# The factor of each RMS norm in a three-layer decoder kernel: square root and reciprocal instead of logarithm and exponential

## The reference

```python
def rmsnorm(x, gain):
    xf = x.astype(jnp.float32)
    y = xf * lax.rsqrt(jnp.mean(xf * xf, axis=-1, keepdims=True) + NORM_EPS)
    return (y * gain.astype(jnp.float32)).astype(x.dtype)
```

## Time and profile before

| | |
|---|---|
| median of 3 runs | 2280.27 us (2279.29 to 2281.51) |
| profiled execution | 2277.27 us |
| its span | 2275.5 us |
| mean granted clock of TensorE | 0.981 |
| busy: PE / DVE / ACT / POOL | 2178.8 / 1092.6 / 767.3 / 1146.0 us |
| share of the chain that ended last: PE / DVE / ACT | 84% / 9% / 3% |

### The profile page before, as it was taken

The page is one execution under the profiler, slowest core; times in us unless marked ns, Lnnn a source line. Parts: engine busy times, 40 slices in busy tenths (PEclk is TensorE's granted clock), DMA queues, the critical chain, the costliest instruction groups (busy, mean ns, idle before and its releaser), DMA issues.

```text
span 2275.5 us, 25960 instructions
## 1 busy us (share of the span) xinstructions
PE 2178.8 (96%) x9850; PEld 1803.8 (79%) x9850; DVE 1092.6 (48%) x1258; ACT 767.3 (34%) x850; POOL 1146.0 (50%) x817
## 2 busy tenths in 40 slices
PE   7999989999999999999999999979999799999996
PEld 5888768888888778978888888768887688888885
DVE  6255645555322356543545522774557655453224
ACT  5223343222123344543222223313565432222232
POOL 4465426555554433326555545535555455555554
PEclk9999999999999999989999999989999899999998
DMA  4211102322233222213232232222222222222331
GB/s 165 75 62 50 56 25 107 108 93 92 94 109 120 74 75 74 70 42 130 93 106 97 92 108 95 93 74 92 93 92 75 90 93 92 97 106 92 111 109 49
DMA packets 30198, 203.16 MB, mean 89 GB/s; under 512 B 3252, under 2 KB 3508, under 8 KB 6200
## 3 DMA queue, kind: packets, MB, share of 16 engines
q1 hardware_dynamic: 30136, 202.29, 25.0%
HBM read 200.18 MB, written 2.10 MB: 89 GB/s over the span
## 4 chain that ended last, share of the span: by engine, by line
PE 84%; DVE 9%; ACT 3%; issue 2%; POOL 0%; DMA 0%; DVEq 0%; ACTq 0%; SPq 0%; POOLq 0%
PE bank L1451 83%; DVE x L1340 1%; ACT L584 1%; ACT rstd L584 1%; DVE aqk L1211 1%; DVE x L1403 1%; DVE m_hi L1415 0%; DVE h L1350 0%; DVE rot L1210 0%; POOL ssq L570 0%; DVE un L1209 0%; ACT w_hi L584 0%; ACT s_a L584 0%; PE bank L1704 0%; DVE un L954 0%
## 5 line engine op out<-in xcount | busy, mean ns | idle before, releaser
L496 POOL TENSOR_TENSOR w_lo<-raw,w_hi 128x512 fp32r<-128x512 f32 x680 | 988.8, 1484 | 962.5 <-ACT w_hi L584 962.5
L1451 PE MATMUL bank<-u_hi,w_hi 128*128 128x512 f32 x1952 | 773.9, 396 | 38.9 <-DVE u_lo L958 15.1
L1451 PE MATMUL bank<-u_lo,w_hi 128*128 128x512 f32 x1952 | 764.1, 391 | 0.0
L584 ACT ACTIVATE w_hi<-raw 128x2048 fp32r<-128x2048 f32 x187 | 357.7, 1913 | 872.0 <-PE bank L1451 867.6
L1451 PE MATMUL bank<-u_hi,w_lo 128*128 128x512 f32 x1952 | 487.0, 389 | 0.0
L1451 PEld LDWEIGHTS bank<-u_hi,w_hi 128*128 128x128 f32 x1952 | 369.5, 189 | 122.9 <-issue 26.2
L1451 PEld LDWEIGHTS bank<-u_lo,w_hi 128*128 128x128 f32 x1952 | 369.4, 189 | 77.8 <-issue 2.6
L1451 PEld LDWEIGHTS bank<-u_hi,w_lo 128*128 128x128 f32 x1952 | 366.6, 188 | 76.4
L1451 PE MATMUL bank<-act_hi,w_hi 128*128 128x512 f32 x528 | 205.4, 389 | 0.0
L1451 PE MATMUL bank<-act_lo,w_hi 128*128 128x512 f32 x528 | 205.4, 389 | 0.0
L979 DVE TENSOR_TENSOR h<-h,bank 128x512 f32<-128x512 f32 x48 | 32.8, 683 | 304.3 <-PE bank L1451 304.3
(11 more groups left out here) (237 smaller groups left out, 2235.9 us busy)
## 6 DMA issues: line engine op xcount, KB each, us to landing
raw<-wall SPq DMA_DIRECT2D x187, 1024.0 KB, 4.8
h<-x_t SPq DMA_DIRECT2D x4, 512.0 KB, 6.9
out_t<-h SPq DMA_DIRECT2D x2, 512.0 KB, 2.8
out_t<-h SPq DMA_DIRECT2D x4, 256.0 KB, 3.0
lmask_f<-lmask_in SPq DMA_DIRECT2D x1, 512.0 KB
cs<-cs_in SPq DMA_DIRECT2D x1, 512.0 KB, 3.5
pf<-p_t SPq DMA_DIRECT2D x1, 512.0 KB, 3.5
amask<-amask_in SPq DMA_DIRECT2D x1, 256.0 KB
```

The source lines that it names most:

```text
L496: ins = nc.gpsimd.tensor_tensor(w_lo[:, s, c], raw[:, s, c], w_hi[:, s, c].bitcast(F32), ALU.subtract)
L584: return nc.scalar.activation(out, in_, func, **k)
L1451: return nc.tensor.matmul(out, lhsT, rhs, start=start, stop=stop, skip_group_check=True)
```

## The change

Each factor is now made by one Sqrt on ACT (`norm_root`) and one reciprocal on DVE (`norm_scale`, in place, DVE). The reciprocals stand in DVE's list right ahead of the first use; for m = 0 and 2 the small one of `rcol` comes first, and ACT takes the root of `rcol` ahead of that of `rstd`. The per-head factors of the recurrence (`root(hd)`) keep their Ln and Exp. The diff, cut to its core:

```diff
-            def norm_scale(m):
+            def root_of_mean(out, total):
+                return af(out, total, ACT.Sqrt, bias=eps[:, 0:1], scale=1.0 / DM)
+
+            def norm_root(m):
                 act.wait_ge(ms_ready, m + 1)
                 if m == TWIN:
-                    ch.link(af(rstd2[:], MS[:], ACT.Ln, bias=eps[:, 0:1], scale=1.0 / DM))
-                    af(rstd2[:], rstd2[:], ACT.Exp, scale=-0.5).then_inc(r4_ready, 1)
+                    root_of_mean(rstd2[:], MS[:]).then_inc(root_ready, 1)
                     act.wait_ge(t5_ready, 1)
-                    ch.link(af(rstd[:], sq[:, 0, :], ACT.Ln, bias=eps[:, 0:1], scale=1.0 / DM))
-                    af(rstd[:], rstd[:], ACT.Exp, scale=-0.5).then_inc(r5_ready, 1)
+                    root_of_mean(rstd[:], sq[:, 0, :]).then_inc(root_ready, 1)
                     return
-                ch.step(af(rstd[:], MS[:], ACT.Ln, bias=eps[:, 0:1], scale=1.0 / DM))
                 if m in (0, 2):
-                    ch.step(af(rcol[:], PB[5][:, 0:2 * TT], ACT.Ln, bias=eps[:, 0:1], scale=1.0 / DM))
-                ch.settle()
-                af(rstd[:], rstd[:], ACT.Exp, scale=-0.5).then_inc(rstd_ready, 1)
-                if m in (0, 2):
-                    ch.link(af(rcol[:], rcol[:], ACT.Exp, scale=-0.5))
+                    root_of_mean(rcol[:], PB[5][:, 0:2 * TT]).then_inc(rcol_root, 1)
+                root_of_mean(rstd[:], MS[:]).then_inc(root_ready, 1)
...
+            def norm_scale(m):
+
+                if m in (0, 2):
+                    dve.wait_ge(rcol_root, m // 2 + 1)
+                    ch.step(nc.vector.reciprocal(rcol[:], rcol[:]))
+                    ch.settle()
+                dve.wait_ge(root_ready, m + 1 if m < TWIN else m + 2)
+                nc.vector.reciprocal(rstd[:], rstd[:]).then_inc(rstd_ready, 1)
+                dve.wait_ge(rstd_ready, m + 1)
+
             def ffn(f, r, m):
-                dve.wait_ge(rstd_ready, m + 1)
+                norm_scale(m)
...
-            dve.wait_ge(r4_ready, 1)
+            dve.wait_ge(root_ready, TWIN + 1)
+            ch.link(nc.vector.reciprocal(rstd2[:], rstd2[:]))
             ch.link(tt(sq[:, 0, :], rstd2[:], rstd2[:], ALU.mult))
             tt(sq[:, 0, :], sq[:, 0, :], PB[5][:], ALU.mult).then_inc(t5_ready, 1)
             ch.link(nc.vector.memset(xpad[:, :, 0:3], 0.0))
-            dve.wait_ge(r5_ready, 1)
+            dve.wait_ge(root_ready, TWIN + 2)
+            ch.link(nc.vector.reciprocal(rstd[:], rstd[:]))
             ch.link(tt(rstd[:], rstd[:], rstd2[:], ALU.mult))
             dve.sem_inc(rstd_ready, 1)
```

More of the change, by code:

```diff
@@ L279, in build @@
         sg_ready = sem("sg_ready")
-        r4_ready = sem("r4_ready")
+        root_ready = sem("root_ready")
         t5_ready = sem("t5_ready")
-        r5_ready = sem("r5_ready")
+        rcol_root = sem("rcol_root")
         fin_ready = sem("fin_ready")
@@ L646, in ffn @@
                     if s == 0:
-                        norm_scale(m)
+                        norm_root(m)
                     act.wait_ge(sgin_ready, FT * f + s + 1)
@@ L669, in _ @@
             conv(1)
-            norm_scale(0)
+            norm_root(0)
             def sigmoids(p):
@@ L693, in by_tokens @@
                 conv(p0 + 2)
+                act.wait_ge(rstd_ready, 1)
                 for t in range(TT):
@@ L792, in values @@
                 act.wait_ge(tok_done, TT * (2 + g) + c + 1)
+                if c == 0:
+                    act.wait_ge(rstd_ready, 3)
                 k = (TT if g else 0) + c
@@ L814, in _ @@
                 if t == 0:
-                    norm_scale(2)
+                    norm_root(2)
                 halves(0, t)
@@ L876, in _ @@
                 if t == 0:
-                    norm_scale(TWIN)
+                    norm_root(TWIN)
             with act.Fori(0, KC // 2) as i:
@@ L931, in _ @@
                 if q == 0:
-                    norm_scale(6)
+                    norm_root(6)
                 for c in range(2):
@@ L939, in _ @@
                 squares(7, j)
-            norm_scale(7)
+            norm_root(7)
         @block.vector
@@ L1058, in _ @@
             cp(lmask[:], lmask_f[:]).then_inc(masks_ready, 1)
-            dve.wait_ge(rstd_ready, 1)
+            norm_scale(0)
             def both_scaled(n, t, ready, before):
@@ L1250, in _ @@
             dve.wait_ge(cs_loaded, 16)
-            dve.wait_ge(rstd_ready, 3)
+            norm_scale(2)
             for a in range(2):
@@ L1419, in _ @@
             ffn(2, 6, 5)
-            dve.wait_ge(rstd_ready, 7)
+            norm_scale(6)
             for q in range(4):
@@ L1442, in _ @@
             dve.wait_ge(gained, KC)
-            dve.wait_ge(rstd_ready, 8)
+            norm_scale(7)
             for j in range(OUT_SPLIT):
```

## The result

The changed kernel takes 2286.03 us in the median of 11 runs (2281.21 to 2290.35), the kernel before 2280.28 (2272.08 to 2282.32). The ratio is 1.0027, 95% interval 1.0018 to 1.0036: slower by 4 to 8 us. A second set of 12 runs gave 2287.02 against 2280.19, ratio 1.0032 (1.0020 to 1.0044).

A forecast was written before the change was run, and what follows sets the result against it. PE bounds the kernel (84% of the chain), so ACT and DVE count only where PE waits or only DVE remains. 1.2 + 1.6 + 1.4 + 1.2 + 0.2 = +5.6 us on 2280.27 gives 2285.9; 8-in-10 range 2281.5 to 2290.0.

The forecast's parts named there:

- The four norms behind which PE or the end waits: Costs at m = 2 (+1.2, clock +1.6), m = 4 (+1.4), m = 7 (+1.2) and m = 0 (+0.2).
- the four that are covered: Norms m = 1, 3, 5, 6: +1.2 us each against 2.9 spare, so no cost.
- The length of a reciprocal: A 128x512 reciprocal on DVE, R, put at 3.1 us between bounds of 0.73 and 5.6.
- the three ways to read the 203 ns: Fixed start from small operation or product, or excess spread over seven columns: R = 2.9 to 3.2, or 3.25 us.
- The short reciprocal: Rival: R = 0.73 us on DVE makes the kernel faster, -4.6 us, 2275.7; chance 0.09.
- the long one: Rival: R = 4.3 us, some 8 ns a column on DVE, +11 us, 2291; chance 0.13.
- The bound of 1.6: At m = 4, POOL may hold up the first reciprocal by up to one slice, 1.6 us; taken as 0.
- The clock behind m = 2: PE's wait grows from 1.03 to 2.2 us, its clock falls: +1.6 (bounds 0 to 1.6), beside +1.2 for path.
- m = 0 (+0.2): First norm: reciprocal and hand-over delay DVE 3.4 us, nearly covered by PE's and POOL's slack; +0.2, bounds 0 to 1.8.
- m = 4 (+1.4): Two factors before the convolution: +2.4 us on DVE, 1.0 returned through less overlap with POOL, +1.4 left.
- m = 7 (+1.2): Last norm, only product and store behind it: 3.1 + 0.1 - 2.05 = +1.2 us.
- The table load: ACT load before Exp costed at 1.28 us, not the skill's 2.66, which would bring the change out near even.

The follow-up runs named there:

- only_m1356: New factor at m = 1, 3, 5 and 6 only, other norms as in the kernel before: 2279.24 against 2279.66 us, ratio 1.0003.
- before_late: Kernel before with only DVE's decay-coefficient chain moved behind the first stage's work: 2279.53 against 2280.19 us, ratio 0.9996.
- the four partial kernels: Kernel before with the new factor only at m = 0, only 4, only 7, or only 1, 3, 5, 6: 2282.29, 2279.84, 2281.80, 2279.24 us.
- only_m2: New factor at m = 2 only, other norms as in the kernel before: 2280.63 us, ratio 1.0009.
- only_m7: New factor at m = 7 only, other norms as in the kernel before: 2281.80 us, ratio 1.0010.
- one_function: Factor by ACT's absolute reciprocal square root alone, DVE reciprocals dropped from the changed kernel: 2275.63 against 2279.66 us for the kernel before, ratio 0.9980.

## Why the prediction was right, and where its terms were off

The sum was +5.6 us and the medians say +5.75 and +6.8. Sign, range and size hold. That 2285.9 met 2286.03 to 0.1 us is luck: two terms were wrong, one 1.6 too high and one 2.8 too low, and the other three lie within 0.2.

- **Where it counts.** The four norms behind which PE or the end waits, and the four that are covered, were read rightly: only_m1356 shows nothing, and m = 2, 4 and 7 each show their step. The choice of the places where something waits, and not ACT's 17.8 us of saved time as a whole, carried the forecast.
- **The length of a reciprocal** was put at 3.1 and is 3.35, 8% more. Of the three ways to read the 203 ns, the one that spread the excess over the columns behind the first (6.0 ns, 3.25 us) came nearest to the 6.26 measured. The short reciprocal (0.73) and the long one (4.3) are both out. It is also the same beside POOL: the one at m = 1 has POOL's slices beside it for 1.9 of its 3.35 us (they start at 371.98 and take 5.00), and all seven are 3353. The bound of 1.6 that I kept for a hold-up was not needed.
- **The clock behind m = 2 (+1.6)** is the term that failed. The step read a rule into two waits of one trace: 1.55 kept the clock, 1.97 lost it. A wait of 2.47 lost it in one profile and kept it in another, and in five profiles where m = 2 is untouched (before_late and the four partial kernels other than only_m2) PE is at half clock just ahead of that place. So the term is the +1.4 of the longer path alone, where the prediction had 1.2 + 1.6 = 2.8. What a longer wait costs in clock is small enough, or random enough, that these runs don't show it.
- **m = 0 (+0.2)** is the other one that failed, and it is 3. I had moved DVE's work as a block from 37.02, taking for granted that it would still arrive there. The change moved ACT's next rounding two microseconds ahead, and with it POOL, on to a chain of small DVE operations. I had looked at POOL behind the norm and not ahead of it. The evidence was in the trace before, in the four operations of 1.14 to 1.22 us behind 28.49. The experiment that moves the chain shows it: the same reciprocal, no wait.
- **m = 4 (+1.4)** held: 1.4 to 1.5 where PE takes up its work behind the convolution, in all four profiles with the new factor there. Its two parts were both short: 2.87 later at the product where 2.4 was said, of which 1.4 and not 1.0 came back. The mechanism, DVE meeting less of POOL's slices, fits the six steps of 4.31 instead of 7.16. What I left out is that the product of the two factors now falls beside POOL (+0.7), which the larger return covers.
- **m = 7 (+1.2)** is 1.4 (1.35 in only_m7, 1.45 in the changed kernel), by the longer reciprocal.
- **The table load.** With 1.28 for a load the steps come out (m = 7: 3.35 + 0.1 - 2.05 = 1.40), and one_function, which has neither Exp nor reciprocal, gains 3.07 at m = 4 over the kernel before as far as the product. The 2.66 for a switch (the Trainium skill, ScalarE: Activation LUTs, section What ACT_TABLE_LOAD costs) would have made the change about even, and no run here bears it out.

With the steps of the profiles the sum is 3.0 + 1.4 + 1.4 + 1.4 = 7.2, inside both intervals (4 to 8 of the first set, 4.6 to 10 of the second). The medians say 5.75 and 6.8 and the means of the same runs 6.7 (2286.36 against 2279.62) and 7.2 (2286.41 against 2279.18): the executions of the kernel before reach further below their median than above it. What is left between 5.75 and 7.2 is within the noise of 11 or 12 runs.

The other 5.7 of the 12.9 between the first two profiles is PE at half clock where the profile before has it at full clock: 1.6 near the second panel, 1.4 behind m = 2, 1.7 near 1000 us in the attention, 0.6 behind the convolution, and the rest in steps of under 0.5. That is argued from the same panels in other profiles. Why one execution has more such stretches than another stays open.

## What to carry to other kernels

Count an exchange of engines at the places where something waits: here ACT was busy 17.8 us less, and only some 2 us at each of four factors counted; of nine reciprocals of 3.35 us on DVE, the four on those paths outweighed that, and a fifth cost 3 us at m = 0 by falling behind a stretched chain. The whole is 6 to 7 us slower. A reciprocal on a whole tile costs about five products of its size (3.35 against 0.69); take it on a small tile (200 ns for eight columns; not tried here for the whole factor), or use a function that makes it unnecessary, which was 4 us faster than the kernel before instead of 6 slower. And when an engine gets shorter, follow the engines it feeds: the work that it releases earlier may land beside something that used to run alone. Finally, read a step where the engine that bounds the stage takes up its work, and not some roundings later, where the clock of the one execution has come in: at m = 4 that is the difference between 1.4 and 2.1.

## What the runs showed of the hardware

- The granted clock of TensorE is not set by the length of the wait ahead alone. Behind a wait of 2.47 us it was 1.00 once and 0.52 once, in the same place of the program. A stretch at half clock costs about 1.6 us where PE sets the pace, and single executions of the kernel before lie between 2270.6 and 2282.4.
- Reciprocal on VectorE took 200 ns for 8 columns and 3353 ns for 512, the same to 1 ns in nine places, alone and with GpSimd at work beside it for up to 1.9 us. Products and scalings of SBUF tiles beside GpSimd took up to 1.51 instead of 0.69, and products and scalings of eight columns 1.2 us instead of 0.17.
